# Row sums every eight key steps, output projection in every key step, spatial mixing under attention

## The reference, cut to what matters

```python
a = rms_norm(h, g_mix);  z = a @ w_in                     # q, k, v, u, v_gmlp: 5120 columns
q, k = apply_partial_rope(q), apply_partial_rope(k)       # 8 heads, two 64-wide components each
s = einsum('bqhcd,bkhcd->bhcqk', q, k) * 64 ** -0.5       # bidirectional
pr = softmax(s);  att = pr[:, :, 0] - lam * pr[:, :, 1]
o = rms_norm(einsum('bhqk,bkhd->bqhd', att, v), g_subln) * (1 - lambda_init)
gm = gelu(u) * (einsum('hpq,bcqhd->bcphd', w_s, layer_norm(gelu(v_gmlp))) + b_s)
h = h + concat([o, gm]) @ w_out
h = h + conv_glu_ffn(rms_norm(h, g_ffn))                  # up 2 x 5632, depthwise conv, silu, down
h = h + (p @ w_ple_up) * sigmoid(rms_norm(h, g_ple) @ w_ple_gate)
return rms_norm(h, g_final)
```

## Time and profile before

| | us |
|---|---|
| median of 3 runs | 2063.35 (2062.81 to 2065.03) |
| profiled execution | 2064.24 |
| its span, slowest core (7) | 2062.7 (others from 2053.6) |
| TensorE busy | 1917.6 (93%) |
| VectorE, ScalarE busy | 999.0, 749.4 |
| first value projection and its end | about 134 to 202 |
| query projection and spatial mixing | 405 to 486 |
| attention without and with fill | 486 to 631, 631 to 922 |
| last block of the output projection | 922 to 982 |

### The profile page before, as it was taken

One profiled execution on the slowest core, in us unless ns is written; L12 is line 12 of the kernel. 1 busy time (PEld: TensorE's weight loads), 2 busy tenths in 40 slices (PEclk: granted clock), 3 DMA queues, 4 the chain that ended last, 5 costly groups with the idle time before them and its releaser, 6 DMA issues.

```text
span 2062.7 us, 31107 instructions; the slowest of 8 cores (2053.6 to 2062.7 us)
## 1 busy us (share of the span) xinstructions
PE 1917.6 (93%) x11708; PEld 1059.0 (51%) x11708; DVE 999.0 (48%) x1305; ACT 749.4 (36%) x1039; POOL 186.3 (9%) x281
## 2 busy tenths in 40 slices
PE   5988999987889999988999999999999999999994
PEld 1433455554445555545666654566654566644441
DVE  3645201254444544554566641366641366643667
ACT  4621111104887777765222210122210022233553
POOL 5600000000000000001000000000000010001000
PEclk9998999999999999999999999999999999999997
DMA  9750344366002333328644444444444464444603
GB/s 223 221 109 14 69 82 62 53 120 195 1 1 42 52 54 60 52 52 134 111 73 75 78 75 75 78 79 75 74 75 78 82 103 77 71 72 83 108 26 138
DMA packets 60371, 170.43 MB, mean 83 GB/s; under 512 B 10816, under 2 KB 15168, under 8 KB 60096
## 3 DMA queue, kind: packets, MB, share of 16 engines
q0 software_dynamic: 34992, 125.58, 36.3%
q1 hardware_dynamic: 25232, 42.86, 6.6%
HBM read 279.29 MB, written 8.39 MB: 139 GB/s over the span
## 4 chain that ended last, share of the span: by engine, by line
PE 81%; DVE 6%; ACT 5%; issue 4%; DMA 3%; SPq 1%; POOL 1%; DVEq 0%; ACTq 0%; POOLq 0%
PE ps L336 81%; ACT big L339 4%; DVE big L342 3%; DMA big<-xo 1%; SPq L559 1%; DVE big L354 1%; DVE big L345 1%; DMA big<-wup 1%; POOL big L349 1%; DVE big L351 1%; DMA big<-xa 0%; DVEq L170 0%; DMA big<-big 0%; DMA big<-posa 0%; DVE big L349 0%
## 5 line engine op out<-in xcount | busy, mean ns | idle before, releaser
L336 PE MATMUL ps<-big 128*128 128x342 bf16 (+3 forms) x11708 | 1917.6, 330 | 125.1 <-ACT big L339 51.0
L336 PEld LDWEIGHTS ps<-big 128*128 128x128 bf16 (+1 forms) x11708 | 1059.0, 98 | 982.1 <-issue 257.9
L339 ACT ACTIVATE big<-big 128x1024 f32<-128x1024 f32 (+8 forms) x547 | 423.4, 792 | 925.8 <-DVE big L342 703.0
L342 DVE TENSOR_TENSOR big<-big 128x342 f32<-128x342 f32 (+8 forms) x424 | 306.1, 735 | 224.0 <-ACT big L339 190.2
L339 ACT ACTIVATE big<-ps 128x684 bf16<-128x684 f32 (+1 forms) x432 | 294.6, 705 | 178.2 <-PE ps L336 173.0
L345 DVE SCALAR_TENSOR_TENSOR big<-big 128x1024 f32<-128x1024 f32 (+1 forms) x228 | 258.5, 1134 | 207.2 <-ACT big L339 197.6
L342 DVE TENSOR_TENSOR big<-ps,big 128x1026 f32<-128x1026 f32 (+4 forms) x239 | 210.7, 897 | 284.1 <-PE ps L336 271.0
L342 DVE TENSOR_TENSOR big<-big,ps 128x342 f32<-128x342 f32 (+1 forms) x96 | 83.1, 866 | 202.6 <-PE ps L336 201.4
L402 POOL DMA_DIRECT2D big<-wup x88 | 46.5, 528 | 539.4 <-PE ps L336 508.7
L339 ACT ACTIVATE big<-ps,big 128x512 bf16<-128x512 f32 x50 | 34.0, 686 | 159.4 <-PE ps L336 159.4
L402 POOL DMA_DIRECT2D big<-wo x48 | 25.5, 532 | 518.5 <-PE ps L336 508.9
(11 more groups left out here) (25 smaller groups left out, 64.5 us busy)
## 6 DMA issues: line engine op xcount, KB each, us to landing
big<-wup POOLq DMA_DIRECT2D x88, 512.0 KB, 5.7
big<-wo POOLq DMA_DIRECT2D x48, 512.0 KB, 5.1
big<-xa SPq DMA_DIRECT2D x32, 512.0 KB, 7.2
big<-wdn POOLq DMA_DIRECT2D x32, 480.0 KB, 5.3
big<-xo SPq DMA_DIRECT2D x16, 512.0 KB, 9.9
big<-wg POOLq DMA_DIRECT2D x16, 512.0 KB, 13.7
y<-big SPq DMA_DIRECT2D x32, 256.0 KB, 2.2
big<-wdn POOLq DMA_DIRECT2D x16, 448.0 KB, 4.9
```

The source lines that it names most:

```text
L336: P.op("pe", lambda e: e.matmul(out, lhsT=lhsT, rhs=rhs, start=start, stop=stop), reads=reads, writes=writes, inc=inc)
L339: P.op("act", lambda e: e.activation(out=out, in_=in_, func=func, **kw), reads=reads, writes=writes)
L342: P.op(en, lambda e: e.tensor_tensor(out=out, in0=a, in1=b, op=op), reads=reads, writes=writes)
```

## The change

- Row sums: 16 matmuls every eighth key step instead of 8 every fourth. The buffers `Pb` grow from 7 to 12; five of them, and the new split buffers, lie in the third blocks of `h` for tiles 0 to 7.
- `sum3` works in bank 6, where the row sums are, and bank 7 belongs to the projection alone. What followed a unit is cut in pieces, each in a key step of its own: norm sum of the unit before the last in step 3, selections in 5 and 7, Ln and Exp of the norm in 6 and 8, one Exp for both components (684 columns) in 10, the products in 11.
- Fill: one or two projection matmuls before and after each value product, 16 in eight steps, none in the eighth, from the middle of unit 9. 48 projection matmuls are left for behind attention (32 before).
- Spatial mixing: three pieces per unit under units 0 to 5, in bank 7.
- The residual comes in pieces during attention; the third blocks of tiles 0 to 7 come behind it. The last block takes tiles 8 to 15 first. Seven weight slots are added, one per unit, in the memory of keys that aren't used any more.
- Last block: bf16 copies of the finished 684 columns are emitted ahead of it; its first six tiles do 15 of 16 products before the last head is needed.
- First value projection: six banks instead of two, halo norm between the two rotary tables.
- Tail: the Ln table is loaded by a one-column activation before it is needed, the last squares are added by a second matmul, and the last products of the first half go behind it.

TensorE, from the query projection to the first attention unit, before: eight query tiles (48 rows of 342 columns each), the 128-column ones are spatial mixing, the 32-row ones row sums.

```diff
-        Pb = [V(o, BF16, 2, NB) for o in [ZT + i * 1368 for i in range(6)] + [ZS + 4104]]
+        ZH = [Z1 + 4104 * j + 2736 for j in range(8)]
+        Pb = [V(o, BF16, 2, NB) for o in [ZT + i * 1368 for i in range(6)] + [ZS + 4104] + ZH[0:5]]
-        S3 = [V(ZRO + i * 684, BF16, NB) for i in range(3)]
-        RS = RM
+        LA = V(ZR, F32, 2, NB)
+        S3 = [[V(ZRO + i * 684, BF16, NB) for i in range(3)], [V(o, BF16, NB) for o in (ZH[5], ZH[5] + 684, ZH[6])]]
+        RS = V(ZH[7], F32, NB)
...
-        for _ in range(3):
+        for _ in range(2):
             WU += [wo_d[t] for t in range(16)]
+        WU += [wo_d[t] for t in list(range(8, 16)) + list(range(8))]
...
             for sl in sls:
-                wfree.append(sl)
+                if not (sl.once and wuse[0] > W_LAST):
+                    wfree.append(sl)
...
-            load_halo(0, 0)
+            load_halo(1, 0)
             yield
-            load_halo(0, 1)
+            load_halo(1, 1)
             yield
-            yield
+            P.inherit(R_tco, R_XS)
+            P.inherit(R_ang, R_XS + R_SQ + [R_ACC[0]])
+            yield from table_steps(0, 1024, TO, roth, R_roth, R_tco)
             halo_norm()
             yield
-            P.inherit(R_tco, R_XS)
-            P.inherit(R_ang, R_XS + R_SQ + R_ACC)
-            yield from table_steps(0, 1024, TO, roth, R_roth, R_tco)
             yield from table_steps(1, NT, (TC, TS), rown, R_rown, R_tca[0])
-        tok_proj(vitems, v_epi(0), [6, 7], hook)
+        tok_proj(vitems, v_epi(0), [6, 7, 0, 1, 2, 3], hook)
...
+        def spatial_mm():
             grp, hh = sp_i[0] // 8, sp_i[0] % 8
-            b = (6, 7)[sp_i[0] % 2]
-            sx, R_sx = SPT[sp_i[0] % 2], R_SPT[sp_i[0] % 2]
+            b = 7
+            sx, R_sx = SPT[sp_i[0] % 2], R_ut[sp_i[0] % 2]
             sp_i[0] += 1
-        SPT = [V(ZRO, F32, 512), V(ZRO + 2048, F32, 512)]
-        R_SPT = [Reg(), Reg()]
+        SPT = [ut[0][:, 0:512], ut[1][:, 0:512]]
...
-            if kt % 4 == 3:
-                for w in range(8):
+            if kt % 8 == 7:
+                for w in range(16):
                     g = w % 4
-                    pp = (k - 3 + w // 2) % NP
-                    pe(ps[32 * g:32 * g + 32, 6, 0:NB], onesb[:, 0:32], Pb[pp][:, w % 2, :], kt == 3 and w < 4, kt == 15 and w >= 4,
-                       [R_P[pp], R_c], [Rb[6]], w == 7)
+                    pp = (k - 7 + w // 2) % NP
+                    pe(ps[32 * g:32 * g + 32, 6, 0:NB], onesb[:, 0:32], Pb[pp][:, w % 2, :], kt == 7 and w < 4, kt == 15 and w >= 12,
+                       [R_P[pp], R_c], [Rb[6]], w == 15)
             if kt == 15:
                 cpy(XO, ps[:, 4:6, 0:NB], [Rb[4], Rb[5]], [R_XO])
-                split3(ps[:, 6, 0:NB], [Rb[6]])
+        def sum3(w, i):
+            for n in range(3):
+                pe(ps[:, 6, 0:NB], w, S3[i][n], n == 0, n == 2, [R_s3[i], R_c], [Rb[6]], n == 2)
+        def post_ln(u, c):
+            sum3(selw[c], 0)
+            act(LA[:, c, :], ps[:, 6, 0:NB], AF.Ln, [Rb[6]], [R_la])
+        def post_exp(u):
+            act(LA, LA, AF.Exp, [], [R_la], scale=-1.0)
+        def post_o(u):
+            tt(OO, XO[:, 0, :], LA[:, 0, :], ALU.mult, [R_XO, R_la], [R_oo])
+            stt(LA[:, 1, :], XO[:, 1, :], neglam, LA[:, 1, :], ALU.mult, ALU.mult, [R_XO, R_lam], [R_la])
+            tt(OO, OO, LA[:, 1, :], ALU.add, [R_la], [R_oo])
+            tt(RM, OO, OO, ALU.mult, [R_oo], [R_rm])
+            split3(RM, [R_rm], 1)
+        def post_b(u):
+            sum3(onesb, 1)
+            tsc(RM, ps[:, 6, 0:NB], 1.0 / 128, EPS, ALU.mult, ALU.add, [Rb[6]], [R_rm])
+        def post_rs(u, i):
+            if i == 0:
+                act(RM, RM, AF.Ln, [], [R_rm])
             else:
+                act(RM, RM, AF.Exp, [], [R_rm], scale=-0.5)
+        def post_out(u):
             b, hh = units[u]
-            lnexp(R0, R_r0)
-            stt(mixA[:, hh, b * NB:(b + 1) * NB], OO, gsubc, R0, ALU.mult, ALU.mult, [R_oo, R_r0, R_lam], [R_qb[hh][b]])
+            stt(mixA[:, hh, b * NB:(b + 1) * NB], OO, gsubc, RM, ALU.mult, ALU.mult, [R_oo, R_rm, R_lam], [R_qb[hh][b]])
...
+        FILL = [1, 1, 1, 1, 2, 1, 1, 1, 1, 1, 1, 2, 1, 1, 0, 0]
+            u, st = k // 16, k % 16
+            if 17 <= u < 24 and st == 0:
+                i = u - 17
+                sl = Slot(Z3 + i * 4096, True)
+                P.inherit(sl.reg, R_kT[0][i] + R_kT[1][i])
+                wfree.append(sl)
+                wonce.append(sl.reg)
+                pump()
             if k < nstep:
                 emit_qk(k)
-            u, st = k // 16, k % 16
-            fl = 9 <= u < 24 and st in (1, 2, 3, 4, 9, 10, 11, 12)
+            fl = 9 * 16 + 8 <= k < nstep
             if fl:
-                fill(gen, 2)
+                fill(gen, FILL[2 * st % 16])
+            if u < 9 and st in (3, 8, 12):
+                if sp_i[0] < 16:
+                    spatial_mm()
+                elif not sp_done[0]:
+                    spatial_halo()
+                    sp_done[0] = True
+                    for r in R_hacc:
+                        P.inherit(r, R_ut)
             ka = k - LAG
             if ka >= 0 and ka % 16 != 0:
                 if ka % 16 == 1:
                     emit_av(ka - 1)
                 emit_av(ka)
             if fl:
-                fill(gen, 2)
+                fill(gen, FILL[2 * st % 16 + 1])
+            if u >= 24:
+                continue
             if u < 23 and st == 9:
                 q_pad(u + 1)
-            if st in (7, 15):
-                flush_sq()
-            if u < 24:
-                if u >= 1 and st == 6:
-                    post_a(u - 1, 0)
-                if u >= 1 and st == 8:
-                    post_a(u - 1, 1)
-                if u >= 1 and st == 14:
-                    post_b(u - 1)
-                if u >= 2 and st == 0:
-                    post_c(u - 2)
-        post_c(22)
-        post_a(23, 0)
-        fill(gen, 16)
-        post_a(23, 1)
-        fill(gen, 16)
-        post_b(23)
-        post_c(23)
-        fill(gen, 1000)
-        flush_sq()
+            if st in (2, 12):
+                flush_sq(1)
+            gate = [R_P[k % NP]]
+            if st == 6:
+                if 1 <= u <= 4:
+                    h_first(u - 1, gate)
+                elif 7 <= u <= 8:
+                    h_first(2 * u - 10, gate)
+                    h_first(2 * u - 9, gate)
+                elif 10 <= u < 14:
+                    h_last(u - 6, gate)
+                    if u == 13:
+                        h_tail(1)
+            if u >= 1:
+                if st == 5:
+                    post_ln(u - 1, 0)
+                if st == 7:
+                    post_ln(u - 1, 1)
+                if st == 10:
+                    post_exp(u - 1)
+                if st == 11:
+                    post_o(u - 1)
+            if u >= 2:
+                if st == 3:
+                    post_b(u - 2)
+                if st == 6:
+                    post_rs(u - 2, 0)
+                if st == 8:
+                    post_rs(u - 2, 1)
+                if st == 9:
+                    post_out(u - 2)
...
+        def hg_copy(j):
+            act(hg[:, j, 0:2 * NB], h[:, j, 0:2 * NB], AF.Copy, [R_h[j][0], R_h[j][1], cr["gcols"]], [R_hg[j]], scale=gcols[:, 1, j:j + 1])
         def late(j, hd):
-            act(hg[:, j, 0:2 * NB], h[:, j, 0:2 * NB], AF.Copy, [R_h[j][0], R_h[j][1], cr["gcols"]], [R_hg[j]], scale=gcols[:, 1, j:j + 1])
-            if j == 0:
+            if j == OJ[0]:
                 act(hacc2, hd, AF.Square, [R_h[j][2]], [R_r1])
             else:
                 act(hq[j % 2], hd, AF.Square, [R_h[j][2]], [R_hq[j % 2]])
-        for _ in wout_gen(2, [0, 1, 2, 3, 4, 5], late):
-            pass
+        lsl = {}
+        def wl(m, n0, n1):
+            j = OJ[m]
+            if n0 == 0:
+                (lsl[m],) = take()
+            sl = lsl[m]
+            wt = V(sl.o, BF16, 16, 128)
+            bk = m % 6
+            for n_ in range(n0, n1):
+                kc = (n_ + 8) % 16
+                src = mixA if kc < 8 else mixG
+                rr = [R_qb[kc][2]] if kc < 8 else [R_u[kc - 8]]
+                pe(ps[:, bk, 0:NB], wt[:, kc, :], src[:, kc % 8, 2 * NB:NT], n_ == 0, n_ == 15, [sl.reg] + rr, [Rb[bk]], n_ in (14, 15))
+            if n1 == 16:
+                release([sl])
+                hd = h[:, j, 2 * NB:NT]
+                tt(hd, hd, ps[:, bk, 0:NB], ALU.add, [Rb[bk]], [R_h[j][2]])
+                late(j, hd)
+        fill(gen, 16)
+        post_b(22)
+        post_rs(22, 0)
+        post_rs(22, 1)
+        post_out(22)
+        fill(gen, 8)
+        post_ln(23, 0)
+        fill(gen, 12)
+        post_ln(23, 1)
+        fill(gen, 1000)
+        for i in range(2):
+            h_last(i, [], R_P)
+        post_exp(23)
+        post_o(23)
+        flush_sq()
+        for j in OJ[:6]:
+            hg_copy(j)
+        for n in range(4):
+            wl(n, 0, 15)
```

(32 more changed lines are left out.)

145 lines of the change are left out of this document (68 added, 77 removed).

## The result

The changed kernel takes 2035.03 us (median of 4 runs, 2033.0 to 2039.0) against 2063.64 for the one before, measured beside it: ratio 0.986, 95% interval 0.985 to 0.988, so 28.6 us (1.4%) faster. Forecast were 1998, with a range of 1980 to 2024. The direction was right, and over half of the gain is missing. (Some executions of most kernels here show the cores of one die, or of both, at a lower clock and a longer time; the ratios leave them out, the medians of the experiments don't.)

What follows compares the result with a forecast made beforehand. TensorE was taken as the bound, with 81% of the chain of waits. Gains of 5 + 20 + 28.8 + 9 + 2.3 = 65.1 us took 2064.2 to 1999.1, or 1998 on the median's scale; range 1980 to 2024.

Steps and rivals of the forecast that it cites:

- D: Attention with fill: 17.4 us a unit in place of 19.4, 252.3 us for 14.5 units.
- Rival 2: Attention with fill: the loop of two score banks limits every step, units stay at 19.4 us; 2027 us, chance 0.10.
- Rival 1: TensorE reaches its count: filled units 16.9, plain 15.3, no waits at bank 7 or last-block banks; 1984 us, chance 0.14.
- Rival 4: Attention: sums and split-sums sharing one bank cost 4.5 us per unit, 108 us over 24 units; 2106 us, chance 0.04.
- C: Attention without fill: 16.8 us per unit with spatial work, 15.6 plain; 139.0 us for 8.5 spacings.
- B: Query projection: spatial mixing leaves it, so attention starts earlier; gain 20 us, bounds 17 and 21.
- A: First value projection: six banks let TensorE run further ahead, key tiles start earlier; gain 5 us, bounds 0 and 8.
- E: Last block, from the last attention unit to the channel mixer: 51 us in place of 59.8; gain 9, bounds 3 and 13.
- Rival 3: Last block isn't earlier: ScalarE's copies only change place, bank waits spread over the tiles; 2007 us, chance 0.09.
- F: Tail: table load under earlier waits, last accumulate as a second f32 matmul pass; gain 2.3 us, bounds 0.5 and 3.

Runs made afterwards that it cites:

- experiments 1 and 2: Changed kernel with fill two key steps later, 2008.2 us; changed kernel with the split of the squares emitted in step 15, behind the residual add, 2000.8 us.
- Experiment 7: Changed kernel with the three spatial pieces of a unit in key steps 4, 6 and 8 in place of 3, 8 and 12: 2029.3 us.
- experiment 5: Changed kernel with each probability buffer waiting only for what lies in its own memory: 2037.7 us.
- Experiment 4: Changed kernel with six gain copies ahead of the last two square sums and the ten late ones spread over the first ten tiles: 2032.6 us.
- the four repairs: Changed kernel with later squares split, reordered last-block copies, narrower probability-buffer waits and spatial pieces in steps 4, 6, 8, all together: 1981.6 us.

## Why the prediction was wrong

**The step that failed is in D**: "in every second tile the next projection matmul comes about 0.4 us too early". I had the right place, bank 7 emptied behind eight operations, and the wrong size: 1.95 us. I summed the eight operations from emission in step 11, 3.9 us. The trace starts them later, when ScalarE's exponential of 684 columns lets the first product go. They then take 5 us, since each is followed by about 0.1 us in which the next hasn't started, and since a ninth, the square sum emitted in step 12, stands among them, which I hadn't counted. A start in step 11 is where the code puts an operation, not where its operands are ready. Forecast for the unit were 17.4; without the wait the runs gave 17.03, and my count of matmuls had said 17.0. Bank 7 was forecast at 0.4 us a unit and cost 2.2: over 14 units 25 us more, two thirds of what is missing. 1.8 of the 2.2 is the wait itself (26.8 us in 14.5 units); the other 0.4 is time at half clock, 5 us in the stretch, which the sum didn't have at all. The unit measured, 19.24, also lies outside the bounds that I had given it, 16.9 and 18.8.

Rival 2 said that spreading the fill brings nothing, 2027 us. It is the nearest in its time and wrong in its mechanism: TensorE waited 0.4 us for ScalarE in the whole stretch, and without the wait for VectorE spreading gave about 0.9 us a unit. Rival 1 (16.9 a unit, nothing at bank 7) describes experiments 1 and 2 to 0.1 us. Rival 4, one bank for sums and split-sums, did not come: in plain units the waits for VectorE are 1.9 us in seven units, against 4.5 before.

**C** came out 2.7 us better than forecast (to the tenth copy, with half a filled unit: 127.9 + 17.1 = 145.0 us against 139.0 + 8.7 = 147.7), as two errors against each other. Plain units take 14.55, not 15.6: I had priced the fewer groups and nothing else, while the new order of the post-processing also took TensorE's waits from 14.9 us in seven units to 7.2. Units with three spatial pieces take 17.35 to 17.71 (second to fourth spacing), not 16.8: I had 0.4 us for VectorE's queue, and it was 1.05 and 1.18 in two places. Experiment 7 removed both, and then the matmuls themselves cost 0.5 to 0.7.

**B**: 14.8 for 20 us. TensorE's first scores come 29 us earlier than in the earlier trace rows (core 4 against core 7), but the next ones wait for ScalarE:

```profile
456.55 0.74 PE L339 MATMUL ps<-big 128*128 128x342 bf16 x4 [3.51 <-DVE big L357]
...
462.25 6.02 PE L339 MATMUL ps<-big 128*128 128x342 bf16 x23 [4.96 <-ACT big L342]
```

Three of the missing are a new wait that experiment 5 shows: with spatial mixing gone nothing lies between the last query transfers and attention, and the buffers' waits for the staging slots, which before had long been over, decide. I had followed what moved away, and not what every buffer inherits. The other two stay open.

**A**: 3.3 for 5 us. The wait for ScalarE stayed, in one piece, 7.28 us (core 4) in place of 5.49 and 2.29 (row below). The forecast's working also has a slip: 192.4 and three evacuations of 0.6 us are 194.2, not 194.9, which would have made the gain 5.8 us.

```profile
190.01 10.18 PE L339 MATMUL ps<-big 128*128 128x512 bf16 x34 [7.28 <-ACT big L342]
```

**E**: 2.1 for 9 us. I had seen the ten copies ahead of the banks' emptying, at 3 us; it was 3.20. I had missed that the square sums emitted first wait 5.55 us for VectorE and hold the six early copies behind them, and that the late chain then ends 3 us behind TensorE (core 4):

```profile
912.00 0.49 ACT L342 ACTIVATE big<-big 128x342 f32<-128x342 f32 x1 [5.55 <-DVE big L345]
```

Experiment 4 gave 6.2 us back. Rival 3, that the copies only change place, was close in its number for the kernel as made, 2 us in place of none, but not in its mechanism: in another order the same copies cost 6 us less.

**F**: 1.6 for 2.3, within its bounds. The table load lies under TensorE's wait, as the step said, and the f32 matmul has four parts in place of two (core 4):

```profile
2008.71 1.28 ACT L342 ACT_TABLE_LOAD   x1
...
2015.15 1.35 ACT L342 ACTIVATE big<-big 128x512 f32<-128x512 f32 x2 [3.61 <-DVE big L354]
```

```profile
2010.50 3.75 PE L339 MATMUL ps<-big 128*128 128x512 f32 x4 [5.11 <-DVE big L345]
```

## What to carry to other kernels

When work is spread into a queue that another engine must empty, find what stands in that engine's queue at the moment of emptying and when its operands are ready, in us from a trace of the neighbouring stage; here the waits in 14 units (26.8 us) cost more than all stage borders together had gained (A, B, E and F, 22 us). Each of the four repairs moved or narrowed a few lines, and together they took off another 53 us, nearly twice what the change itself had gained. Moved work is not hidden work: moved spatial mixing cost 12.7 of the 16.1 us it saved, and 2.3 when its steps were chosen by where VectorE is idle (118.1 against 115.8 us for the first nine copies).
